# A two-layer recurrent and windowed-attention step on one core: input norm from a second copy of the input, sample states two slots earlier, fp32 scores, and sixteen low parts on another engine

## Chip, cores and metric

One core of one Trainium2 chip. The metric is the device time of one execution in microseconds (us), lower is better. Before the change the median of 3 runs is 1066.13 us (1063.52 to 1066.85).

## What is computed

A prompt of 1024 tokens and 8 single sample tokens (T = 1032 columns, 1024 features) go through two layers. Layer 1 is HGRN2, a gated linear recurrence with 8 heads of 128 x 128 state; layer 2 is attention over a window of 128 with 16 query heads, 2 key/value heads and learned sinks. Both have a SiLU gate path and a residual.

```python
u = _rmsnorm(h, norm_g) @ w_in
q, f, i, g = split(u)                       # layer 1
S = exp(b_end) * S + einsum(k * exp(b_end - b), v);  o = q_decayed @ S + masked(q k^T) v
h = h + (rmsnorm(o) * silu(g)) @ w_out
s = einsum(q, k) * scale                    # layer 2, banded blocks of 128 queries, 256 keys
m = max(max(s), sink);  p = exp(s - m);  o = p @ v / (sum(p) + exp(sink - m))
h = h + (o * silu(gate)) @ w_out2;  y = rmsnorm(h)
```

The outputs are y, the recurrent states of prompt and samples, and the last keys and values.

## The kernel before, in words

Features lie on the 128 partitions and tokens along them. A weight block of 128 x 1024 (`n`, 0 to 73) is multiplied with the stream in three units of 344 columns (`TU`), each unit in one PSUM bank. To keep fp32 accuracy at the speed of the one-pass type fp32r, weights and stream are each cut into a high part and a low part, and a unit is 24 products: 8 feature tiles times (high x high, high x low, low x high). The high part of a weight block is made on ACT (`prepare`, L782), the low part on POOL for early blocks (L643) and on DVE for late ones (L1095, L1100). The unit banks are G0 to G2; `start_unit` (L1582) waits until the former content of the bank was read (`unit_read`). The other five banks, R0 to R4, serve everything else.

Every engine runs a list written out by hand, and semaphores connect them. In the order of time:

**Start (0 to 39 us).** SP loads the input `x` in 8 feature tiles of 516 KB into A, weight blocks between them. For each tile ACT squares it (L878), PE sums the squares over the partitions by 3 plain fp32 products with a matrix of ones (L1691), DVE makes XH (L1220) and XL (L1222), and PE does the 9 products of block 0 (L1696). After the last tile ACT turns the sums into 1/rms, `RB` (L886, L889), and DVE multiplies each unit by it when it reads its bank (`evacuate`, L1103). So no bank of block 0 can be emptied, and block 1 can't start, before RB is there.

**Recurrence (39 to 475 us).** Iterations `it` = 0 to 8 of 9 slots, one unit per slot, while the recurrence of head it - 1 is worked on in the same slots: `diagonal`, six `level`s, transposes in slots 2 and 7, `chunk_sums` in slot 8 on PE. In slot 8 DVE runs `decode_state` (L1168: products of sample values and keys, its input read at a stride of 8 elements), `decode_add` (L1177) and then `chunk_states` (L1183: 8 dependent steps). Slot 0 of the next iteration has `head_output` (L1660) on PE, which needs those chunk states. The sample values are stored to DRAM by SP (L495) and read back to all partitions (L499). POOL decays the sample states in slot 4 (`decode_parts`, L677).

**Middle (475 to 784 us).** Gate blocks, output projection, residual, shared keys and values, queries with rotation. ACT makes KBH (L969) and DVE KBL (L1362), the high and low parts of the rotated keys.

**Attention (784 to 1001 us).** Steps s = -3 to 31; query group q is 2 head pairs x 128 queries. PE's order in a step is `values(s-1)`, `turn(s)`, `scores(s+2)`, then 17 products of gate blocks (s < 16) or 18 of the first half of the output projection (s from 16, L1842). ACT cuts the queries (L1002), DVE makes their low part (L1414), PE multiplies three fp32r combinations into two banks (L1788), using the upper and the lower 64 rows of the array for the two heads of a pair. DVE's `minima` (L1417) adds the mask, ACT takes the exponentials (L1009), DVE the denominators, POOL normalises (L716). For s from 17, `cut_slice` cuts the gated outputs of 16 groups: ACT the high part (L1025), DVE the low one (L1456).

**End (1001 to 1061 us).** Second half of the output projection, final norm, store.

Of the kernel before, what the change touches and what calls it, by code (L numbers as in the profile page):

```python
# [20 lines left out]
D = 1024  # L21
# [65 lines left out]
def unit_bank(u):  # L87

    return u % (2 if NU * N_B2 <= u < NU * N_BO else 3)
# [38 lines left out]
def build(nc, ctx, ins, outs):  # L128
# [3 lines left out]
    x_d, w_d, gain_d, lbl_d, st_d, lmask_d, imask_d, ident_d, cs_d, amask_d, smask_d, sink_d, sinks_d, kc_d, vc_d = ins  # L132
    y_d, stp_d, sts_d, kwin_d, vwin_d = outs
    h1_d = nc.dram_tensor("h1_spill", [P, KT, T], fp32, kind="Internal").ap()
    vs_d = nc.dram_tensor("sample_values", [HEADS, P, DEC], fp32, kind="Internal").ap()
# [54 lines left out]
    SQT = (VD, VK, KTT)  # L190
# [10 lines left out]
    KBH, KBL = sb("KBH", [P, SEQ], fp32r, rb_), sb("KBL", [P, SEQ], fp32r, rb_)  # L201
    rfree = [rb_[0]]
# [10 lines left out]
    QNH, QNL = sb("QNH", [P, 2, 2, P], fp32r, rb_), sb("QNL", [P, 2, 2, P], fp32r, rb_)  # L213
# [27 lines left out]
    R = [ctx.enter_context(nc.psum_tensor(f"R{i}", [P, 512], fp32)) for i in range(NBANK_R)]  # L241

# [8 lines left out]
    x_split = sem("x_split")  # L251
    sq_done = sem("sq_done")
    sq_used = sem("sq_used")
    ln_done = sem("ln_done")
    rb_done = sem("rb_done")
# [54 lines left out]
    kb_high = sem("kb_high")  # L310
# [32 lines left out]
    qn_high = sem("qn_high")  # L343
    qn_done = sem("qn_done")
# [111 lines left out]
    def _(sp):  # L456
# [10 lines left out]
        sp.dma_start(gain[:], gain_d).then_inc(const_in, 16)  # L467
        for k in range(KT):
            sp.dma_start(A[:, k, :], x_d[:, k, :]).then_inc(x_in[k], 16)
            if k < 3:  # L470
                load_weights(k)
            if k == 1:
# [19 lines left out]
        def sample_values(r):  # L492

            sp.wait_ge(unit_read, 9 * r + 9)
            sp.dma_start(vs_d[r], RAWV[:, SEQ:T]).then_inc(vs_out, 16)  # L495
            if r:
                sp.wait_ge(ss_prod, 2 * r)
            sp.wait_ge(vs_out, 16 * (r + 1))
            sp.dma_start(VD[:, 0:SEQ], vs_d[r].rearrange("e b -> (e b)").unsqueeze(0).broadcast_to([P, SEQ])  # L499
                         ).then_inc(vd_in, 16)  # L500
# [133 lines left out]
    def _(pool):  # L634
# [129 lines left out]
    def _(act):  # L764
# [31 lines left out]
        def gates(h):  # L796
# [10 lines left out]
            else:  # L807
                act.wait_ge(sq_used, KT)
# [65 lines left out]
        for k in range(KT):  # L874
            act.wait_ge(x_in[k], 16)
            if k >= 3:
                act.wait_ge(sq_used, k - 2)
# [3 lines left out]
        act.wait_ge(lbl_diff, 1)  # L881
        nc.scalar.activation(lbw[:, 1], lbw[:, 1], ACT.Exp).then_inc(lbl_exp, 1)
        act.wait_ge(setup_dve, 1)
        act.wait_ge(sq_used, KT)
        for i in range(NU):
            ins = nc.scalar.activation(RB[:, seg(i)], R[i][:, 0:TU], ACT.Ln, scale=1.0 / D, bias=eps[:])  # L886
        ins.then_inc(ln_done, 1)
        act.wait_ge(ln_done, 1)
        nc.scalar.activation(RB[:], RB[:], ACT.Exp, scale=-0.5).then_inc(rb_done, 1)  # L889
        nc.scalar.preload_act_table_set("sigmoid_and_others")  # L890

        for it in range(HEADS + 1):
            p, r = it - 2, it - 1
            for slot in range(9):
                if slot % 3 == 0:
# [73 lines left out]
        nc.scalar.activation(KBH[:], KE[:, 0:SEQ], ACT.Copy).then_inc(kb_high, 1)  # L969
# [25 lines left out]

        def cut_queries(q):

            if q == 0:
                act.wait_ge(q_rot, HP)
            if q >= 2:  # L1000
                act.wait_ge(sc_done, 2 * (q - 1))
            nc.scalar.activation(QNH[:, q % 2], pair(A, q), ACT.Copy, scale=-1.0).then_inc(qn_high, 1)  # L1002
# [24 lines left out]
        for s in range(-3, NQ + 1):  # L1027
            if 0 <= s < NQ:
                copy_before(s)
            if s + 3 < NQ:  # L1030
                cut_queries(s + 3)
# [60 lines left out]
    def _(dve):  # L1092
# [10 lines left out]
        def evacuate(u, i, dst):  # L1103
            dve.wait_ge(unit_done, u + 1)
            nc.vector.tensor_tensor(dst[:, seg(i)], G[i][:, 0:TU], RB[:, seg(i)], ALU.mult).then_inc(unit_read, 1)  # L1105
# [62 lines left out]
        def decode_state(r):  # L1168
            for i in range(2):
# [3 lines left out]
                                        VD[:, 0:SEQ].rearrange("p (e b) -> p b e", b=DEC)[:, 4 * i:4 * i + 4],  # L1173
# [39 lines left out]
        nc.vector.memset(ones[:], 1.0)  # L1213
        nc.vector.memset(eps[:], EPS).then_inc(setup_dve, 1)
        nc.vector.memset(AT[:], 0.0).then_inc(setup_dve, 1)
        dve.wait_ge(const_in, 16)
        for k in range(KT):
            g = gain[:, GAIN_A, k:k + 1]
            dve.wait_ge(x_in[k], 16)
            nc.vector.tensor_scalar(XH[:, k, :], A[:, k, :], g, None, ALU.mult).then_inc(x_split, 1)  # L1220
            dve.wait_ge(x_split, 2 * k + 1)
            nc.vector.scalar_tensor_tensor(XL[:, k, :], A[:, k, :], g, XH[:, k, :].bitcast(fp32), ALU.mult, ALU.subtract  # L1222
                                           ).then_inc(x_split, 1)
# [10 lines left out]
        dve.wait_ge(rb_done, 1)  # L1234
# [3 lines left out]
        for it in range(HEADS + 1):  # L1238
            r = it - 1
            for slot in range(9):  # L1240
# [10 lines left out]
                if r >= 0:  # L1251
# [109 lines left out]
        dve.wait_ge(kb_high, 1)  # L1361
        nc.vector.tensor_tensor(KBL[:], KE[:, 0:SEQ], KBH[:].bitcast(fp32), ALU.subtract).then_inc(kb_done, 1)  # L1362
# [48 lines left out]
        def cut_queries(q):  # L1411

            dve.wait_ge(qn_high, q + 1)
# [564 lines left out]
```

## Time and profile before

| | |
|---|---|
| median of 3 runs | 1066.13 us |
| profiled execution | 1063.2 us, its span 1061.4 us |
| PE busy | 1010.1 us, 95% of the span |
| DVE / POOL / ACT busy | 631.4 / 428.8 / 386.8 us |
| mean granted TensorE clock | 0.991 of full |

In the profile PE is TensorE's matmuls, PEld its weight loads, DVE the vector engine, ACT the scalar engine, POOL GpSimd, SP the queue that issues DMAs. A plain fp32 matmul shows as two instructions, an fp32r one as one. L1592 is a line of the kernel before. Idle time in brackets stands with the engine that ended it.

### The profile page before, as it was taken

The page shows a single profiled execution, that of the slowest core. Times are in us where ns is not written, and L with a number is a line of the kernel's source. Part 1 is how long each engine was busy: PE and PEld are TensorE (multiplying, and loading weights), DVE is VectorE, ACT ScalarE, POOL GpSimd, SP SyncE. Part 2 cuts the span into 40 slices and gives each one's busy share as a digit, 9 for nine tenths or more (in the row PEclk, how much of TensorE's full clock was granted, in tenths as well). Part 3 has the DMA queues.
Part 4 walks back from the last instruction along what each step waited for, and adds up shares of the span by engine and source line. Part 5 has one row for each costly group of instructions (what it writes and reads, how often), then busy time and mean ns, then how long its engine had stood idle before and what let it go on. Part 6 is the DMA issues. An engine that isn't in the chain of part 4 may idle for free.

```text
span 1061.4 us, 22401 instructions
## 1 busy us (share of the span) xinstructions
PE 1010.1 (95%) x9360; PEld 944.2 (89%) x9360; DVE 631.4 (59%) x1195; ACT 386.8 (36%) x775; POOL 428.8 (40%) x286
## 2 busy tenths in 40 slices
PE   6999999999999999999999999999989999898996
PEld 4899999999999998899999999999988888777895
DVE  8153746555564737456743234367667878977835
ACT  4412313132313133545332233510047757654522
POOL 1244545545545454612135342344535334322243
PEclk9999999999999999999999999999989989999998
DMA  7111213030312222012233324211112113322103
GB/s 284 41 61 41 86 39 104 21 104 24 102 63 64 71 73 83 22 43 63 103 105 136 120 80 145 77 46 58 40 57 63 59 56 101 91 71 61 50 34 127
DMA packets 50533, 81.39 MB, mean 77 GB/s; under 512 B 15425, under 2 KB 34433, under 8 KB 50305
## 3 DMA queue, kind: packets, MB, share of 16 engines
q1 hardware_dynamic: 50432, 79.97, 23.1%
q8 instruction: 74, 1.21, 0.5%
q14 instruction: 27, 0.21, 0.1%
HBM read 62.35 MB, written 17.60 MB: 75 GB/s over the span
## 4 chain that ended last, share of the span: by engine, by line
PE 71%; DVE 15%; ACT 7%; issue 5%; POOL 1%; DMA 0%; DVEq 0%; SPq 0%; ACTq 0%; POOLq 0%
PE G L1592 51%; PE G L1842 5%; DVE SP L1429 4%; ACT SP L1009 4%; PE R L1645 3%; DVE VK L1172 3%; DVE QNL L1414 3%; PE R L1691 2%; PE R L1619 1%; PE R L1684 1%; PE R L1670 1%; DVE PT L1447 1%; PE R L1667 1%; PE G L1696 1%; PE R L1631 1%
## 5 line engine op out<-in xcount | busy, mean ns | idle before, releaser
L1592 PE MATMUL G<-XH,WH 128*128 128x344 f32 x1176 | 385.8, 328 | 1.9 <-DVE RAWF L1105 1.9
L1592 PE MATMUL G<-XL,WH 128*128 128x344 f32 x1176 | 378.0, 321 | 2.4 <-DVE KE L1399 1.9
L1592 PE MATMUL G<-XH,WL 128*128 128x344 f32 x744 | 237.7, 319 | 0.0
L1592 PEld LDWEIGHTS G<-XH,WH 128*128 128x128 f32 x1176 | 221.9, 189 | 6.0 <-issue 2.4
L1592 PEld LDWEIGHTS G<-XL,WH 128*128 128x128 f32 x1176 | 221.7, 189 | 5.0 <-DVE WL L1095 2.2
L643 POOL TENSOR_TENSOR WL<-WR,WH 128x1024 fp32r<-128x1024 f32 x40 | 104.3, 2608 | 178.8 <-ACT WH L782 178.8
L782 ACT ACTIVATE WH<-WR 128x1024 fp32r<-128x1024 f32 x58 | 61.1, 1055 | 261.1 <-PE G L1592 166.7
L1592 PEld LDWEIGHTS G<-XH,WL 128*128 128x128 f32 x744 | 139.8, 188 | 0.0
L1592 PE MATMUL G<-XL,WL 128*128 128x344 f32 x432 | 139.2, 322 | 0.0
L674 POOL TENSOR_TENSOR K<-K,FP 128x512 f32<-128x512 f32 x48 | 78.1, 1627 | 104.6 <-PE R L1645 104.6
L720 POOL TENSOR_TENSOR SP<-SP,small 128x1024 f32<-128x1024 f32 (+1 forms) x32 | 57.3, 1792 | 135.1 <-DVE small L1440 135.1
L1009 ACT ACTIVATE SP<-SP,small 128x256 f32<-128x256 f32 (+1 forms) x128 | 61.8, 484 | 68.0 <-DVE small L1429 68.0
L1592 PEld LDWEIGHTS G<-XL,WL 128*128 128x128 f32 x432 | 81.9, 190 | 0.4
L1105 DVE TENSOR_TENSOR RAWQ<-G,RB 128x344 f32<-128x344 f32 x27 | 14.0, 517 | 79.7 <-PE G L1592 79.7
L1592 PE MATMUL G<-GR,WL 128*128 128x344 f32 x192 | 61.4, 320 | 0.0
L1592 PE MATMUL G<-GR,WH 128*128 128x344 f32 x192 | 61.4, 320 | 0.0
L1592 PE MATMUL G<-AR,WH 128*128 128x344 f32 x192 | 61.3, 319 | 0.0
L1105 DVE TENSOR_TENSOR RAWV<-G,RB 128x344 f32<-128x344 f32 x27 | 14.0, 517 | 77.4 <-PE G L1592 77.4
L1429 DVE CUSTOM_DVE_ANT_0 SP<-R,amask,sink 128x256 f32<-128x256 f32 (+1 forms) x128 | 51.9, 457 | 1.7 <-PE R L1788 1.7
L1842 PE MATMUL G<-XL,WH 128*128 128x344 f32 x144 | 47.9, 333 | 0.8 <-DVE AR L1549 0.8
L736 POOL TENSOR_TENSOR KE<-KE,CS 128x1032 f32<-128x1032 f32 x8 | 27.2, 3395 | 48.0 <-DVE KE L1403 48.0
L1842 PE MATMUL G<-XL,WL 128*128 128x344 f32 x144 | 46.0, 319 | 0.0
(251 smaller groups left out, 1940.6 us busy)
## 6 DMA issues: line engine op xcount, KB each, us to landing
WR<-w SPq DMA_DIRECT2D x58, 512.0 KB, 3.5
A<-x SPq DMA_DIRECT2D x8, 516.0 KB, 8.6
RESO<-x SPq DMA_DIRECT2D x8, 516.0 KB, 4.6
h_spill<-H SPq DMA_DIRECT2D x8, 516.0 KB, 2.9
gate_spill<-EV SPq DMA_DIRECT2D x24, 172.0 KB, 1.9
RES<-h_spill SPq DMA_DIRECT2D x24, 172.0 KB, 2.6
y<-H SPq DMA_DIRECT2D x24, 172.0 KB, 1.9
SS<-states SPq DMA_DIRECT2D x8, 512.0 KB, 5.0
```

Source lines behind the costliest of these rows:

```text
L643: nc.gpsimd.tensor_tensor(WL[:, n % 3], WR[:, n % 3], WH[:, n % 3].bitcast(fp32), ALU.subtract).then_inc(lo_pool, 1)
L674: nc.gpsimd.tensor_tensor(low, low, decay(l, 1).unsqueeze(2).broadcast_to([P, SEQ // (2 * h), h]), ALU.mult).then_inc(upd_k, 1)
L720: nc.gpsimd.tensor_tensor(sp_, sp_, small[:, q % 2, 4, :].unsqueeze(2).broadcast_to([P, 4, keys.stop - keys.start]), ALU.mult).then_inc(p_ ...
L782: nc.scalar.activation(WH[:, n % 3], WR[:, n % 3], ACT.Copy).then_inc(hi_done, 1)
L1009: nc.scalar.activation(SP_[q % 2][:, i, keys], SP_[q % 2][:, i, keys], ACT.Exp, bias=sm[:, 0, i:i + 1], scale=-1.0, accum_out=sm[:, 2, i:i ...
L1105: nc.vector.tensor_tensor(dst[:, seg(i)], G[i][:, 0:TU], RB[:, seg(i)], ALU.mult).then_inc(unit_read, 1)
L1172: nc.vector.tensor_tensor(VK[:, half(i)].rearrange("p (b e) -> p b e", b=4), VD[:, 0:SEQ].rearrange("p (e b) -> p b e", b=DEC)[:, 4 * i:4 ...
L1414: nc.vector.scalar_tensor_tensor(QNL[:, q % 2], pair(A, q), -1.0, QNH[:, q % 2].bitcast(fp32), ALU.mult, ALU.subtract).then_inc(qn_done, 1)
L1429: ins = nc.vector.tensor_tensor_reduce(out=SP_[q % 2][:, i, keys], in0=ps[:, keys], in1=amask[:, keys], scale=1.0, scalar=sink[:, h + i:h ...
L1592: return nc.tensor.matmul(G[unit_bank(NU * n + i)][:, 0:TU], w[:, n % 3, k, :], x[:, seg(i)], start=(k == 0 and p == 0), stop=(k == KT - 1 ...
L1645: ins = nc.tensor.matmul(b[v * w:v * w + w - h, first // 2:(first + w) // 2].rearrange("p (n h) -> p n h", h=h), K[r % 2][:, first:first + ...
L1842: return nc.tensor.matmul(G[unit_bank(u)][:, 0:TU], wt[:, k, :], x, start=(w == 0), stop=(w == 11))
```

## The change

- **Input norm.** A second, token-major copy of the input (`xt`, 8 tiles of 128 tokens x 1024, and `xs` for the samples) is loaded after the first. ACT squares each tile with a running sum along the row (one sum per token), then Ln and Exp give 1/rms with tokens on the partitions; PE's new `spread_scale` turns these 9 columns into rows on all partitions by 9 small fp32 products in slot 5 of iteration 0, and ACT copies them into RB. The 24 fp32 products with ones go. XH of tiles 1 to 7 moves from DVE to ACT. Weight block 0 is loaded ahead of the input, and PE starts when its high part is there; the low x high products run one tile later. Units 3 to 5 (block 1) go to R2 to R4 through the list `U`, so that they need no emptied bank.
- **Sample states.** `decode_state` and `decode_add` run in slot 6, `chunk_states` stays in slot 8 and comes first there. The sample values are stored transposed (pieces of 4 bytes) so that DVE reads them contiguously.
- **Scores.** One plain fp32 product per head in place of three fp32r ones, straight from the rotated queries and a negated copy of the keys (KNEG, made by ACT). The query cuts on ACT and DVE and KBL go.
- **Low parts.** `cut_slice`'s low part moves from DVE to POOL, behind `normalise` of the same step.

```diff
 def unit_bank(u):
+    if u < 2 * NU:
+        return u
@@ start, DMA queue
+        load_weights(0)
         for k in range(KT):
             sp.dma_start(A[:, k, :], x_d[:, k, :]).then_inc(x_in[k], 16)
-            if k < 3:
-                load_weights(k)
+        load_weights(1)
+        for c in range(NC):
+            sp.dma_start(XT[c][:, 0:D], xt_d[:, c]).then_inc(xt_in[c], 16)
+            if c == 3:
+                load_weights(2)
+        sp.dma_start(XS, xs_d).then_inc(xs_in, 16)
@@ sample_values
-            sp.dma_start(vs_d[r], RAWV[:, SEQ:T]).then_inc(vs_out, 16)
+            sp.dma_start(vs_d[r].rearrange("b e -> e b"), RAWV[:, SEQ:T], allow_slow_non_contiguous=True).then_inc(vs_out, 16)
@@ POOL, attention
-        for s in range(-3, NQ):
+        for s in range(-3, NQ + 1):
             if 0 <= s + 1 < NQ:
                 normalise(s + 1)
+            if s >= 17:
+                cut_slice(s - 1)
@@ ACT, start
-        for k in range(KT):
-            nc.scalar.activation(SQT[k % 3][:], A[:, k, :], ACT.Square).then_inc(sq_done, 1)
-            if k < 2:
-                prepare(k)
+        prepare(0)
+        for k in range(1, KT):
+            act.wait_ge(x_in[k], 16)
+            nc.scalar.activation(XH[:, k, :], A[:, k, :], ACT.Copy, scale=gain[:, GAIN_A, k:k + 1]).then_inc(x_hi_act, 1)
+        prepare(1)
+        for c in range(NC):
+            act.wait_ge(xt_in[c], 16)
+            nc.scalar.activation(XT[c][:, 0:D], XT[c][:, 0:D], ACT.Square, accum_out=SUM[:, c:c + 1]).then_inc(sq_done, 1)
+            if c == 0:
+                act.wait_ge(lbl_diff, 1)
+                nc.scalar.activation(lbw[:, 1], lbw[:, 1], ACT.Exp).then_inc(lbl_exp, 1)
+            if c == 5:
+                prepare(2)
...
+        nc.scalar.activation(SUM, SUM, ACT.Ln, scale=1.0 / D, bias=eps[:]).then_inc(ln_done, 1)
+        nc.scalar.activation(RSTD, SUM, ACT.Exp, scale=-0.5).then_inc(rstd_done, 1)
+        for i in range(2):
+            act.wait_ge(spread, i + 1)
+            nc.scalar.activation(RB[:, half(i)], R[i][:], ACT.Copy).then_inc(rb_done, 1)
@@ DVE, recurrence
                     if slot == 8:
+                        chunk_states(r)
+                    if slot == 6:
                         decode_state(r)
                         decode_add(r)
-                        chunk_states(r)
@@ PE, start
+        def spread_scale():
+            pe.wait_ge(rstd_done, 1)
+            pe.wait_ge(masks_in, 16 * 3)
+            for c in range(NC):
+                ins = nc.tensor.matmul(R[c // 4][:, (c % 4) * P:(c % 4 + 1) * P], RSTD[:, c:c + 1].broadcast_to([P, P]),
+                                       ident[:], start=True, stop=True)
...
+            pe.wait_ge(rb_done, 1)
+            nc.tensor.matmul(R[0][:, 0:DEC], RSTD[0:DEC, NC:NC + 1].broadcast_to([DEC, P]), ident[0:DEC, 0:DEC],
+                             start=True, stop=True).then_inc(spread, 1)
...
+                if it == 0 and slot == 5:
+                    spread_scale()
@@ PE, scores
-                for n, (a, k) in enumerate(((QNH, KBH), (QNH, KBL), (QNL, KBH))):
-                    for v in range(2):
-                        ins = nc.tensor.matmul(R[v][:, 2 * P * jj + keys.start:2 * P * (jj + 1)], a[rows, q % 2, jj, :],
-                                               k[rows, tok], start=(n == 0), stop=(n == 2))
+                for v in range(2):
+                    ins = nc.tensor.matmul(R[v][:, 2 * P * jj + keys.start:2 * P * (jj + 1)], pair(A, q)[rows, jj],
+                                           KNEG[rows, tok], start=True, stop=True)
```

## Rows read from the trace of the kernel before

**Rows 1.** The page, chain that ended last: shares of the span by engine and line.
```profile
PE G L1592 51%; PE G L1842 5%; DVE SP L1429 4%; ACT SP L1009 4%; PE R L1645 3%; DVE VK L1172 3%; DVE QNL L1414 3%; PE R L1691 2%; PE R L1619 1%; PE R L1684 1%; PE R L1670 1%; DVE PT L1447 1%; PE R L1667 1%; PE G L1696 1%; PE R L1631 1%
```
**Rows 2.** PE's waits: who for whom: us in total, times, longest.
```profile
PE R L1670 <- DVE ST L1192: 6.9, 8, 1.0
...
PE R L1788 <- DVE small L1429: 10.2, 13, 1.2
PE R L1788 <- DVE QNL L1414: 3.8, 1, 3.8
PE R L1815 <- DVE PT L1447: 1.6, 2, 1.0
PE G L1842 <- DVE AR L1549: 0.8, 1, 0.8
```
**Rows 3.** The chain in order of time, start-up: start us, us, what.
```profile
34.42 1.75 PE R L1691 x6
...
39.47 26.68 PE G L1592 x168
```
**Rows 4.** Timeline of the start: start us, us, engine, instruction, idle before it.
```profile
6.58 1.06 ACT L782 ACTIVATE WH<-WR 128x1024 fp32r<-128x1024 f32 x1 [0.23 <-DMA WR<-w]
...
10.26 2.56 POOL L643 TENSOR_TENSOR WL<-WR,WH 128x1024 fp32r<-128x1024 f32 x1 [0.20 <-ACT WH L782]
...
10.65 3.26 DVE L1222 SCALAR_TENSOR_TENSOR XL<-A,gain,XH 128x1032 fp32r<-128x1032 f32 x1
...
14.61 1.30 DVE L1222 SCALAR_TENSOR_TENSOR XL<-A,gain,XH 128x1032 fp32r<-128x1032 f32 x1
```
**Rows 5.** Stretches: busy of PE, PEld, DVE, ACT, POOL; PEclk, DMA share, GB/s.
```profile
10.00:12.00 2.00, 1.84 (x3) 1.17 (x4) 1.96 (x2) 1.24 (x2) 1.80 (x2) 1.00 1.04 422
...
38.00:40.00 2.00, 0.53 (x3) 0.56 (x4) 1.19 (x3) 1.98 (x2) 0.00 (x0) 1.00 0.00 0
...
780.00:784.00 4.00, 1.27 (x12) 1.27 (x12) 3.42 (x4) 2.24 (x5) 0.60 (x1) 0.77 0.01 2
```
**Rows 6.** Timeline around the end of iteration 4: DVE, then PE.
```profile
249.92 0.52 DVE L1105 TENSOR_TENSOR RAWV<-G,RB 128x344 f32<-128x344 f32 x1 [2.63 <-PE G L1592]
...
255.07 4.23 DVE L1172 TENSOR_TENSOR VK<-VD,K 128x512 f32<-128x512 f32 x2
259.34 1.89 DVE L1180 TENSOR_TENSOR SS<-SS,VK 128x1024 f32<-128x1024 f32 x1
...
261.46 2.72 DVE L1195 SCALAR_TENSOR_TENSOR ST<-ST,DECC,R 128x128 f32<-128x128 f32 x7
...
261.48 0.49 PE L1670 MATMUL R<-QU,ST 128*128 128x128 f32 x2 [0.94 <-DVE ST L1192]
```
**Rows 7.** Timeline of the same iteration: an issue of SP, and POOL in slot 4.
```profile
220.60 0.38 SPq L481 DMA_DIRECT2D SS<-states  x1
...
237.95 1.90 POOL L680 TENSOR_TENSOR SS<-SS,DECC 128x1024 f32<-128x1024 f32 x1
```
**Rows 8.** Timeline of one attention step, PE.
```profile
927.00 0.39 PE L1788 MATMUL R<-KBH,QNH 64*128 64x256 f32 x2 [0.79 <-DVE small L1429]
...
927.91 0.43 PE L1842 MATMUL G<-XL,WXH 128*128 128x344 f32 x1
...
930.94 1.08 PE L1815 MATMUL R<-PT,VP 128*64 128x256 f32 x8
931.95 1.09 PE L1800 MATMUL R<-ident,SP 128*128 128x128 f32 x8
```
**Rows 9.** Timeline of the same step, DVE.
```profile
930.32 1.42 DVE L1414 SCALAR_TENSOR_TENSOR QNL<-A,QNH 128x256 fp32r<-128x256 f32 x1
```
**Rows 10.** The chain in order of time, 784 us.
```profile
784.27 6.14 PE G L1592 x24
```
**Rows 11.** Weight loads of the recurrence by form: busy us, mean ns; idle before.
```profile
L1592 PEld LDWEIGHTS G<-XH,WH 128*128 128x128 f32 x577 | 108.5, 188 | 2.8 <-issue 0.2
...
L1667 PEld LDWEIGHTS R<-AT,VH 128*128 128x128 f32 x128 | 19.1, 191 | 0.0
```

More of the change, by code:

```diff
@@ L200, in build @@
     rb_ = [rest]
-    KBH, KBL = sb("KBH", [P, SEQ], fp32r, rb_), sb("KBL", [P, SEQ], fp32r, rb_)
-    rfree = [rb_[0]]
+    KNEG = sb("KNEG", [P, SEQ], fp32, rb_)
+    rb_[0] += 4 * SEQ
     rb_[0] += 2 * 4 * SEQ
@@ L212, in build @@
     PT = sb("PT", [P, 2, 512], fp32, rb_)
-    QNH, QNL = sb("QNH", [P, 2, 2, P], fp32r, rb_), sb("QNL", [P, 2, 2, P], fp32r, rb_)
+    rb_[0] += 2 * 4 * 4 * P
     SGR = sb("SGR", [P, 2, 2, P], fp32, rb_)
@@ L250, in build @@
     lb_done = sem("lb_done")
-    x_split = sem("x_split")
+    xt_in = [sem(f"xt_in{c}") for c in range(NC)]
+    xs_in = sem("xs_in")
+    x_hi_dve = sem("x_hi_dve")
+    x_hi_act = sem("x_hi_act")
+    x_lo = sem("x_lo")
     sq_done = sem("sq_done")
-    sq_used = sem("sq_used")
     ln_done = sem("ln_done")
+    rstd_done = sem("rstd_done")
+    spread = sem("spread")
     rb_done = sem("rb_done")
@@ L872, in gate_sigmoid @@
             nc.scalar.activation(SG[m % 2][:], GT[m][:], ACT.Sigmoid).then_inc(g_sig, 1)
[L874 removed]
+        prepare(0)
+        act.wait_ge(const_in, 16)
+        for k in range(1, KT):
             act.wait_ge(x_in[k], 16)
[L876 to L889 removed]
+            nc.scalar.activation(XH[:, k, :], A[:, k, :], ACT.Copy, scale=gain[:, GAIN_A, k:k + 1]).then_inc(x_hi_act, 1)
+        prepare(1)
+        act.wait_ge(setup_dve, 1)
+        for c in range(NC):
[6 more added lines that the diff above has]
+                prepare(2)
+        act.wait_ge(xs_in, 16)
+        nc.scalar.activation(XS, XS, ACT.Square, accum_out=SUM[0:DEC, NC:NC + 1]).then_inc(sq_done, 1)
+        act.wait_ge(sq_done, NC + 1)
+        nc.scalar.activation(SUM, SUM, ACT.Ln, scale=1.0 / D, bias=eps[:]).then_inc(ln_done, 1)
+        act.wait_ge(ln_done, 1)
+        nc.scalar.activation(RSTD, SUM, ACT.Exp, scale=-0.5).then_inc(rstd_done, 1)
+        for i in range(2):
+            act.wait_ge(spread, i + 1)
+            nc.scalar.activation(RB[:, half(i)], R[i][:], ACT.Copy).then_inc(rb_done, 1)
+        act.wait_ge(spread, 3)
+        nc.scalar.activation(RB[:, SEQ:T], R[0][:, 0:DEC], ACT.Copy).then_inc(rb_done, 1)
         nc.scalar.preload_act_table_set("sigmoid_and_others")
@@ L894, in _ @@
             for slot in range(9):
-                if slot % 3 == 0:
+                if slot % 3 == 0 and (it or slot):
                     prepare(3 * it + slot // 3 + 2)
@@ L968, in _ @@
         act.wait_ge(k_rot, 1)
-        nc.scalar.activation(KBH[:], KE[:, 0:SEQ], ACT.Copy).then_inc(kb_high, 1)
+        nc.scalar.activation(KNEG[:], KE[:, 0:SEQ], ACT.Copy, scale=-1.0).then_inc(kb_done, 1)
         for i in range(2):
@@ L994, in _ @@
             prepare(N_BQ + j + 2)
[L996 to L1002, printed above, removed]
         def exponentials(q):
@@ L1409, in _ @@
         dve.wait_ge(q_rot, HP)
-        def cut_queries(q):
-            dve.wait_ge(qn_high, q + 1)
-            nc.vector.scalar_tensor_tensor(QNL[:, q % 2], pair(A, q), -1.0, QNH[:, q % 2].bitcast(fp32), ALU.mult,
-                                           ALU.subtract).then_inc(qn_done, 1)
         def minima(q):
@@ L1684, in head_sums @@
                 nc.tensor.matmul(b[:, 0:TU], ones[:], SQN[:, seg(i)], start=True, stop=True).then_inc(group_done, 1)
+        def spread_scale():
[4 more added lines that the diff above has]
+                                       ident[:], start=True, stop=True)
+                if c % 4 == 3:
+                    ins.then_inc(spread, 1)
+            pe.wait_ge(rb_done, 1)
+            nc.tensor.matmul(R[0][:, 0:DEC], RSTD[0:DEC, NC:NC + 1].broadcast_to([DEC, P]), ident[0:DEC, 0:DEC],
+                             start=True, stop=True).then_inc(spread, 1)
         pe.wait_ge(setup_dve, 1)
-        pe.wait_ge(*lo_value(0))
+        pe.wait_ge(hi_done, 1)
         for k in range(KT):
-            pe.wait_ge(sq_done, k + 1)
+            pe.wait_ge(x_lo, k + 1)
             for i in range(NU):
-                ins = nc.tensor.matmul(R[i][:, 0:TU], ones[:], SQT[k % 3][:, seg(i)], start=(k == 0), stop=(k == KT - 1))
-            ins.then_inc(sq_used, 1)
-            pe.wait_ge(x_split, 2 * k + 2)
-            for i in range(NU):
-                for p, (w, x) in enumerate(((WH, XH), (WH, XL), (WL, XH))):
-                    ins = nc.tensor.matmul(G[i][:, 0:TU], w[:, 0, k, :], x[:, k, seg(i)],
-                                           start=(k == 0 and p == 0), stop=(k == KT - 1 and p == 2))
-                if k == KT - 1:
-                    ins.then_inc(unit_done, 1)
+                for p in range(2):
+                    product(0, i, k, p)
+            if k == 1:
+                pe.wait_ge(*lo_value(0))
+            if k:
+                for i in range(NU):
+                    product(0, i, k - 1, 2)
+        for i in range(NU):
+            product(0, i, KT - 1, 2).then_inc(unit_done, 1)
         for it in range(HEADS + 1):
```

66 lines of the change are left out of this document (32 added, 34 removed).

## Prediction

> **What bounds the kernel now.** I read the page's chain first [rows 1]: the three-product units on PE (L1592, L1842) hold 56% of the span, so PE's own work is most of it, and time can be won only where PE idles, where its clock is low, or where its work shrinks. PE's waits [rows 2] then name the idle places that this change touches: 6.9 us in 8 waits of `head_output` for the first chunk state, 10.2 us before the scores for `minima`, 1.6 us for a copy of turned probabilities, 0.8 us for a low part, and 3.8 us once before the first scores. The start is the last place: PE has 8 groups of fp32 sums there, each like the last one, 1.75 us, and from its end at 36.17 us to 39.47 us PE stands still while ACT makes RB [rows 3].
>
> **Part 1, the start.** I compare when unit 6, the first of block 2, can begin. Before: 39.47 us plus units 3, 4, 5. Seven units take 26.68 us [rows 3], 3.81 each, 0.159 per product, so 50.9 us.
>
> After, one step behind the other. Weight block 0 comes first, the input tile second, so both are there when the first two were before, near 6.5 us [rows 4]. A tile of 516 KB at 422 GB/s [rows 5] takes 1.25 us; DVE's low part takes 1.30 us, and 3.26 us when POOL's low part of a weight block runs beside it (10.65 beside 10.26) [rows 4]. Eight low parts with their gaps are 10.6 us, the first high part 0.75 (an estimate from the length of the same tile), and POOL's two weight blocks each add 2.0: 6.55 + 15.4 = 22.0 us. ACT's high parts, 1.07 to 1.2 us a tile, keep ahead of that. PE has 9 products, 1.43 us, per tile and follows; 12 products are left after the last tile, so block 0 ends at 23.9 us. Units 3 and 4 go into free banks and end at 31.5 us.
>
> RB now hangs on ACT. After the input DVE clears AT and subtracts the small table (1.1 us, an estimate from the 1.30 us of a low part), so ACT passes its wait behind the first square at about 23.3 us. Seven squares with a running sum (1.16 each, by the 1.06 us of a copy of 1024 columns [rows 4] and a tenth for the sum), a weight block (1.06), the sample tile (1.16) and Ln and Exp (0.6) make 10.9 us: 34.2 us. The token-major tiles are no later than that: 9.99 MB stand before the end of the last one, 24 us at 422 GB/s, done at 26 us. So PE idles from 31.5 to 34.2 us, then has 8 small fp32 products of 128 columns (0.22 each by the sums' 0.58 for 344), a wait for ACT's first copy that ends with them, and one tiny product: 36.3 us. Unit 5 ends at 40.1 us, and unit 6 begins: its bank was read long before. **Gain 10.8 us.** From here on iteration 0 has its old order; POOL's and ACT's work for blocks 3 to 5 hangs on PE's units and moves with them.
> Bounds: if ACT never waits for the table, PE is never short and unit 6 starts at 35 us, gain 15.9. If DVE is 3 us later than worked out and the clock is lost in the new idle time (below, 2.4 us), gain 5.4.
>
> **Part 2, sample states.** At the end of iteration 4 DVE spends 4.23 us on the strided products and 1.89 us on the sum before its eight chunk states (a copy, then 2.72 us), and PE waits 0.94 us [rows 6]. With them gone from slot 8, the states start at 255.2 us and end at 258.2 us, before PE ends the next unit at 259.9 us. The wait goes in all 8 iterations: **gain 6.9 us** [rows 2]. What is late next is `diagonal`, which waits for a product of DVE that itself waits for PE; that does not move. In slot 6 DVE idles 2.63 us [rows 6]; contiguous products would take 0.6 us each (half of the 1.30 us of 1032 columns [rows 4]), with 1.2 to 1.9 us for the sum, 2.4 to 3.1 in all: at most 0.5 us late for the next evacuation, which three banks cover. If that cover were gone each iteration would lose the 0.5 us, 4 us. The scattered store is SP's: behind it stand the read-back and the load of the states (220.60), whose user is POOL at 237.95 [rows 7]. Some 17 us lie between, and a load of this size (tile of 516 KB, 1.25 us by the rate) needs a third of them at most: 12 us are free. A store in pieces of 4 bytes shows in no row; I cost it at nothing up to those 12 us.
>
> **Part 3, scores and low parts.** In a step of the second half of this stage PE's groups are scores 0.91 us (927.00 to 927.91), products to 930.94, values 1.01, transposes 1.09, together 6.04 us, and a wait of 0.79 us for DVE: a period of 6.83 us [rows 8]. DVE's ring is: `minima`, wait for ACT's exponentials, denominators, gate, copy, QNL 1.42 us [rows 9], low part, next `minima`. The last two before it go, and the ring falls below 5.41 us, less than PE's 6.04. So PE's waits for DVE in this stage, 10.2 + 1.6 + 0.8 = 12.6 us [rows 2], go; I leave 2 us of them at the two ends: **gain 10.6 us** (12.6 less 2). POOL gets a product of 256 columns behind its normalising; POOL idles over half of the step, and the reader of the low part comes 15 us later.
> The new score group is 4 plain fp32 matmuls of 256 columns on 64 rows each. No row shows such a shape. Nearest are the values: 4 fp32 matmuls of 256 columns in tiles of 64 columns, 8 instructions, 931.95 - 930.94 = 1.01 us [rows 8], which is two at a time: one alone is 0.43 us by the sums, three of 344 columns in 1.75 us [rows 3]. Scores now run two heads at a time as well: 12 instructions in 0.91 us. I take 1.01 for 28 groups (+2.8 us) and half of it for the 4 with 128 keys (-1.6): **loss 1.2 us**. Bounds: below nothing, -2 us, if the mode changes cost less too; and 1.72 us a group if the row halves don't overlap in fp32, a loss of some 21 us.
> The first scores need the last rotated query alone, not its two cuts: **gain 1.0 us** of the 3.8 us wait. In that wait the granted clock falls from 2.4 to 1.2 GHz (0.77 over 780 to 784) [rows 5], and the next unit takes 6.14 us [rows 10] in place of 3.81. PE's idle time of 3.3 us around 38 us left the clock at 1.00 [rows 5]. The new one is 2.8 us, so I take it that the clock stays: **gain 2.4 us** (from 0). KBL goes from DVE at a time when PE runs on, at no gain.
> A rule speaks against the fp32 scores. Fp32 weights of 128 columns load in 191 ns, those of fp32r in 188 [rows 11], and either is hidden behind the matmul before it. The Trainium skill (TensorE: Matmul & The Clock Gate, section on weight-path modes) says that the fast load is on for 128 weights only if the type isn't fp32, and gives about 2x as measured. By it the 8 loads of a group would cost twice as much, an estimate of 1.5 us more a group if nothing hid them. I go by the rows.
>
> **Sum**, against the profiled execution of 1063.2 us (span 1061.4): -10.8 - 6.9 - 10.6 + 1.2 - 1.0 - 2.4 = -30.5, 1032.7 us. The median of the runs shown, 1066.13, lies 2.9 above that execution; on its scale it is 1035.6. I say 1035.
>
> **Rivals.**
> (a) The row halves take turns in fp32: a score group costs 1.72 us. PE is then the bound of every step with 6.85 us (6.04 + 0.81), the idle time is still gone, and about 20 us come back: 1055 us. For it: no row has this shape. Against: the row halves overlap in fp32r, column halves in fp32 [rows 8]. 12%.
> (b) The start pays less, because ACT and DVE are later than worked out or the clock falls in the new idle time: 1041 us. For it: ACT's chain is long and has only estimates for the running sum. 12%.
> (c) The other side: in fp32 neither half of the rows overlaps, nor is a load hidden behind the matmul before it. A group is then 8 loads of 0.19 us and 8 half-matmuls of 0.22 us, 3.2 us, 2.3 more in 32 groups: +72 us, 1105 us. It ends slower from 1.9 us a group on (0.91 plus 31.7 us over 32). Its place would be the score groups alone. 3%.
> (d) Sample states come late: the scattered store takes over 12 us, POOL waits in slot 4, and each us beyond costs 8: at 2 us beyond 1051 us. For it: no row has pieces of 4 bytes. Against: 12 us are free [rows 7]. 3%.
> (e) DVE's freed time doesn't reach PE, since POOL's products delay DVE: a low part of DVE took 3.26 us beside POOL against 1.30 alone [rows 4], and QNL starts while POOL normalises. But `minima` and the copy read PSUM, and PE has 0.6 us to spare against the ring; half of the 10.6 us would be lost, 1040 us. 7%.
> (f) All three gains are hidden by something that I didn't see: no change, 1%.
>
> **How the numbers follow.** The forecast has 62%, and its own range is 1026 to 1044 (the bounds of part 1, the clock, 2.6 us of scatter between runs). With (b), (e) and a part of (d) the range of 8 in 10 is 1024 to 1052; (a) and (c) are mostly left out. A measurement of this kernel tells 0.3%, about 3 us, from no change. Slower by that: (c) and half of the rest of doubt, 4%. Within it: 2%. Faster: 94%.
>
> **What would show it.** Right: unit 6 begins near 40 us, with an idle time of 2 to 3 us ahead of the small products; no wait of L1670's counterpart; score groups of 1.0 us at a period of 6.1 us and no waits for `minima`; granted clock 1.00 at 784 us. Wrong: score groups of 1.7 us or more; PE short before block 1; a wait of DVE in slot 6 for the read-back; idle time of the same length ended by another engine.

## The result and the profile after

The changed kernel takes **1054.16 us** (median of 4 runs, 1051.98 to 1057.27) beside 1066.35 for the kernel before on the same chip: ratio 0.9905, 95% interval 0.9885 to 0.9925. That is faster, but by 1% and not by the 3% that I forecast, and it lies outside my range on the high side. (The quotient of the two medians is 0.989.) The profiled execution, the slowest of the four, took 1057.27 us with a span of 1055.5, against 1061.4 before.

PE's waits in the kernel after, the answer to [rows 2] (columns as there):

```profile
PE R L1652 <- issue: 10.7, 8, 2.5
PE G L1598 <- DVE XL L1243: 10.3, 1, 10.3
PE G L1598 <- issue: 4.6, 6, 1.6
PE R L1638 <- issue: 4.0, 8, 1.5
PE R L1811 <- DVE A L1429: 2.9, 1, 2.9
PE R L1691 <- ACT K L867: 2.2, 1, 2.2
```

The row of 10.3 us is the time before PE's first product. The waits for the first chunk state, for `minima` and for the copy of probabilities are gone, as forecast. In their place stand 15.3 us of "issue" in L1652 (the level products) and L1598 (the three-product units): idle time before an instruction that waited for nothing the profile shows. Before, their counterparts (L1645, L1592) had no such row. L1691 (head sums) waits once for ACT, which is new too.

Three marks cut the span: the first `diagonal` product, the first scores, and the end.

| | before | after | difference | forecast |
|---|---|---|---|---|
| start of the span to the first `diagonal` | 67.66 | 55.20 | -12.5 | -10.8 |
| from there to the first scores | 715.07 | 731.89 | **+16.8** | -7.9 |
| from there to the end | 278.7 | 268.4 | -10.3 | -11.8 |

So the start and the attention stage did what they were to do, and the recurrence took it back. The start, from the chain in order of time of the kernel after, answers to [rows 3]:

```profile
12.89 16.50 DMA VH<-xt
29.42 1.15 ACT VH L901 x2
...
32.24 2.05 PE R L1698 x16
...
34.61 3.98 PE R L1598 x24
38.59 15.11 PE G L1598 x96
```

PE's wait for Ln and Exp is down to 0.6 us, and unit 6 begins at 38.59 us. The chain now starts from the last token-major tile, which lands at 29.4 us; ACT waited 0.75 us for it.

One attention step, the chain of the kernel after, answers to [rows 8]:

```profile
927.96 1.06 PE R L1811 x8
929.02 3.02 PE G L1865 x18
...
934.09 1.06 PE R L1811 x8
```

A score group takes 1.06 us, a step 6.13, and PE idles nowhere in it. The recurrence is where to look. This is its chain over two slots of one iteration:

```profile
206.17 0.89 PE R L1638 x63
207.05 4.04 PE G L1598 x24
211.09 0.88 issue
211.97 0.72 PE R L1652 x48
212.69 3.98 PE G L1598 x24
...
218.35 0.63 PE G L1598 x4
218.98 1.64 issue
220.63 3.30 PE G L1598 x20
```

A unit waits for semaphores only ahead of its first product, yet here one stands still for 1.64 us between its fourth and fifth product. POOL stands still in these slots too. Its product that waits for `diagonal` could start when that ended, at 207.1 us, and started at 210.34 (POOL's timeline; in the version below without the scattered store it starts 0.1 us behind `diagonal`):

```profile
210.34 1.53 POOL L686 TENSOR_TENSOR K<-K,FG 128x512 f32<-128x512 f32 x1 [6.83 <-remote]
```

SP's issues around it, in the kernel after:

```profile
201.76 0.79 SPq L507 DMA_DIRECT2D sample_values<-RAWV  x1
211.71 0.32 SPq L511 DMA_DIRECT2D VD<-sample_values  x1
```

The store of the sample values, whose pieces are now 4 bytes, is the one transfer between: 10 us pass until SP may read back. And the stretches of that time (columns as in [rows 5]):

```profile
204.00:206.00 2.00, 1.81 (x28) 1.42 (x26) 0.63 (x2) 0.81 (x3) 0.00 (x0) 1.00 0.76 184
206.00:208.00 2.00, 1.83 (x70) 1.80 (x71) 1.97 (x5) 0.26 (x1) 0.00 (x0) 1.00 0.00 0
...
210.00:212.00 2.00, 1.12 (x12) 0.83 (x11) 1.50 (x4) 0.00 (x0) 1.53 (x1) 1.00 0.00 0
```

The records of the transfers end by 206 us, the store's semaphore comes at 211.7, and PE and POOL lose time in between, PE again at 219 us. That is the suspicion which the runs test.

The stalls cost more than their own length. In the recurrence of the kernel after, the granted clock fell from 2.4 to 1.2 GHz four times, at 162.0, 264.4, 319.0 and 370.2 us, for 3.4 us each, each time within 1.1 us of the end of such a stall. The first of these stretches, behind a stall that ended at 161.2 us:

```profile
162.00:166.00 4.00, 4.00 (x17) 4.00 (x18) 1.86 (x2) 0.00 (x0) 1.81 (x1) 0.57 0.90 262
```

The seven periods from `diagonal` to `diagonal` are 48.9, 50.4, 51.6, 51.1, 52.3, 53.4 and 52.2 us after, and 49.5 each before. In sum they take 360.0 us after and 346.4 before.

### The profile page after: what moved, and what is told of

The parts are those of the page before. It is cut to its first block, busy times and chain, and to the rows that moved or that the text cites. A ratio compares the mean times of both kernels' runs of the same rounds, so it can differ in the third digit from the quotient of the medians.

```text
span 1055.5 us, 22018 instructions
## 1 busy us (share of the span) xinstructions
PE 1008.5 (96%) x9202; PEld 941.9 (89%) x9202; DVE 563.6 (53%) x1140; ACT 386.8 (37%) x761; POOL 425.8 (40%) x302
## 4 chain that ended last, share of the span: by engine, by line
PE 87%; ACT 3%; issue 3%; DVE 2%; DMA 2%; POOL 1%; SPq 1%; DVEq 0%; POOLq 0%
PE G L1598 57%; PE G L1865 9%; PE R L1652 3%; PE R L1811 3%; PE R L1838 3%; PE R L1823 3%; DMA VH<-xt 2%; PE R L1626 1%; PE R L1674 1%; PE R L1663 1%; PE R L1677 1%; PE R L1691 1%; PE R L1638 1%; POOL WR L649 1%; SPq L482 1%
## 5 line engine op out<-in xcount | busy, mean ns | idle before, releaser
L1598 PE MATMUL G<-XH,WH 128*128 128x344 f32 x1176 | 390.4, 332 | 12.0 <-DVE XL L1243 10.3
L1598 PE MATMUL G<-XL,WH 128*128 128x344 f32 x1176 | 381.8, 325 | 4.9 <-issue 2.6
L1598 PEld LDWEIGHTS G<-XH,WH 128*128 128x128 f32 x1176 | 225.3, 192 | 17.0 <-issue 14.2
L1598 PE MATMUL G<-XH,WL 128*128 128x344 f32 x744 | 237.4, 323 | 0.3 <-issue 0.3
L1598 PEld LDWEIGHTS G<-XL,WH 128*128 128x128 f32 x1176 | 225.3, 192 | 6.8 <-issue 3.6
L1598 PEld LDWEIGHTS G<-XH,WL 128*128 128x128 f32 x744 | 141.4, 191 | 3.1 <-issue 3.0
L1598 PE MATMUL G<-XL,WL 128*128 128x344 f32 x432 | 140.0, 324 | 0.0
L1598 PEld LDWEIGHTS G<-XL,WL 128*128 128x128 f32 x432 | 82.6, 191 | 0.9 <-issue 0.7
L1598 PE MATMUL G<-AR,WH 128*128 128x344 f32 x192 | 61.3, 319 | 0.0
L1598 PE MATMUL G<-GR,WH 128*128 128x344 f32 x192 | 61.3, 319 | 0.0
L1598 PE MATMUL G<-GR,WL 128*128 128x344 f32 x192 | 61.3, 319 | 0.0
L1444 DVE CUSTOM_DVE_ANT_0 SP<-R,amask,sink 128x256 f32<-128x256 f32 (+1 forms) x128 | 52.2, 463 | 12.9 <-PE R L1811 12.5
L1652 PEld LDWEIGHTS R<-QU,K 128*30 128x30 f32 (+5 forms) x2432 | 33.5, 107 | 21.7 <-issue 21.6
L1123 DVE TENSOR_TENSOR RAWQ<-G,RB 128x344 f32<-128x344 f32 x24 | 12.4, 516 | 71.7 <-PE G L1598 71.7
L1652 PE MATMUL R<-QU,K 128*30 128x16 f32 (+5 forms) x2432 | 38.6, 187 | 10.7 <-issue 10.7
L748 POOL TENSOR_TENSOR KE<-KE,CS 128x1032 f32<-128x1032 f32 x8 | 27.2, 3395 | 49.5 <-DVE KE L1424 49.5
```

The lines of the kernel that those rows point to most:

```text
L1444: ins = nc.vector.tensor_tensor_reduce(out=SP_[q % 2][:, i, keys], in0=ps[:, keys], in1=amask[:, keys], scale=1.0, scalar=sink[:, h + i:h ...
L1598: return nc.tensor.matmul(U[unit_bank(NU * n + i)][:, 0:TU], w[:, n % 3, k, :], x[:, seg(i)], start=(k == 0 and p == 0), stop=(k == KT - 1 ...
L1652: ins = nc.tensor.matmul(b[v * w:v * w + w - h, first // 2:(first + w) // 2].rearrange("p (n h) -> p n h", h=h), K[r % 2][:, first:first + ...
```

## The experiments

**The 32-byte store.** Theory A: the store in pieces of 4 bytes holds back instructions of all engines. Everything else of the change stays, the values are stored as before, and DVE reads them with a stride, still in slot 6.

```diff
-            sp.dma_start(vs_d[r].rearrange("b e -> e b"), RAWV[:, SEQ:T], allow_slow_non_contiguous=True)
+            sp.dma_start(vs_d[r], RAWV[:, SEQ:T])
...
-                                        VD[:, half(i)].rearrange("p (b e) -> p b e", b=4),
+                                        VD[:, 0:SEQ].rearrange("p (e b) -> p b e", b=DEC)[:, 4 * i:4 * i + 4],
```

> The changed kernel with the store of sample values in pieces of 32 bytes and the strided products of before, still in slot 6. Theory A (the store in pieces of 4 bytes, 10 us long, holds back the fetching of instructions, which the trace shows as waits called issue in the middle of units): the waits of PE called issue in the recurrence fall from some 15 us to about 4 (those ahead of the diagonal), an iteration takes 48.6 us, and the time is 1034 us. Theory B (the move of decode_state to slot 6 itself delays PE): the strided products take 6.1 us there in place of 2.7, so the waits stay or grow, 1055 us or more. Theory C (the new order at the start shifts what is fetched when): no change, 1054 us.

Measured: 1034.77 us (1032.81 to 1036.88), ratio 0.9728 [0.9712, 0.9745]. PE's waits in it:

```profile
PE G L1598 <- DVE XL L1243: 10.3, 1, 10.3
PE R L1638 <- issue: 4.0, 8, 1.5
PE R L1691 <- ACT K L867: 3.1, 1, 3.1
PE R L1811 <- DVE A L1429: 2.9, 1, 2.9
```

The "issue" rows of L1652 and L1598 are gone, and every period is 48.27 to 48.30 us, 338.0 in sum. One store was worth some 20 us. The periods are 22.0 us shorter in sum than in the kernel after. PE's stalls in them there add up to 14.6 us; four falls of the clock, at half the speed for 3.4 us, are another 6.8 us (an estimate from those lengths): 21.4 together. SP reads back 4.1 us after the store's issue in that iteration (3.3 to 4.6 in the eight).

**The scattered store alone**, in the kernel before: the same diff the other way round, with the decode left in slot 8.

> The kernel before with the store in pieces of 4 bytes and contiguous products alone, still in slot 8. Theory A: 6.9 us are won, since the chunk states begin 3.4 us earlier, and some 20 us are lost to late instructions: about 1079 us, with waits called issue in each iteration. Theories B and C: the win alone, 1059 us.

Measured: 1066.97 us (10 runs, 1061.25 to 1073.27), ratio 1.0041 [1.0017, 1.0065]; the profiled execution is the slowest of the ten, its span 1071.4 against 1061.4. It has a new row:

```profile
PE R L1645 <- issue: 11.3, 8, 2.0
```

The direction is A's, and the row is the one of the kernel after; the size is not. The median is 4 us slower where I expected 16, and the runs scatter over 12 us. The gain that I expected is there: PE's 6.9 us of waits for the first chunk state are not in this version's list, since the contiguous products are shorter and lie ahead of them. So the store costs about 11 us here by the medians, less than the 20 in the kernel after, and some 17 in the profiled execution (10.0 us of span and the 6.9): 11.3 of stalls and three falls of the clock. Why it is less I can't say.

**A scratch store nobody waits for.** To the 32-byte version comes a second store of the same values, in 4-byte pieces, into scratch memory; only the end of the kernel and the next overwriting of its source, most of an iteration later, wait for it.

```diff
+            sp.dma_start(du_d[r].rearrange("b e -> e b"), RAWV[:, SEQ:T], allow_slow_non_contiguous=True).then_inc(v_out, 16)
```

> e1 with one more store in pieces of 4 bytes per head, to a scratch tensor, issued behind the read-back; nothing on the way to the result waits for it, save the overwriting of its source a slot cycle later. Theory A: the late instructions come back whole, some 20 us above e1. Rival A2 (what hurt was that SP stood waiting for the long store, so that the read-back and the load of the states were late): as e1, within 3 us.

Measured: 1062.56 us (9 runs, 1058.14 to 1071.38), ratio 1.0001 [0.9966, 1.0036], 28 us above the version without it. Its row in PE's waits:

```profile
PE R L1655 <- issue: 18.2, 11, 3.4
```

So it isn't that SP or DVE wait for the values. The store itself does the harm, as A says. (DVE's wait ahead of the overwriting is no other cause: it stands in the same place in the versions with 8-byte pieces below, which lose nothing.)

**What about the store does it: four more versions** of the 32-byte kernel, each with one more transfer of small pieces per iteration. First the same 1024 values in 512 pieces of 8 bytes:

```diff
+            sp.dma_start(du_d[r].rearrange("j e i -> e j i"), RAWV[:, SEQ:T].rearrange("e (j i) -> e j i", i=2),
+                         allow_slow_non_contiguous=True).then_inc(v_out, 16)
```

> As e3 (e1 and a scratch store behind the read-back), but in 512 pieces of 8 bytes in place of 1024 of 4. If the price goes with the number of pieces: half of e3's 28 us above e1, 1048 us. If it goes with the bytes or with there being one more store at all: as e3, 1062 us. If pieces of 8 bytes are no longer slow: as e1, 1035 us.

Measured: 1036.38 us, ratio 0.9718 [0.9692, 0.9744]: nothing lost. Then a second read of the sample outputs in 1024 pieces of 4 bytes:

```diff
+            sp.dma_start(QS[:, p, 0, :], os_d[p].rearrange("n e -> e n"), allow_slow_non_contiguous=True).then_inc(os_in, 16)
```

> e1 with the read of sample outputs, 1024 pieces of 4 bytes from DRAM, issued twice (the second into a tile that is free there). It lands in 2.3 us where the store took 10. If small pieces as such hold back instructions: 10 us or more above e1. If only slow stores do: within 3 us of e1, 1035 us.

Measured: 1033.13 us, ratio 0.9708 [0.9678, 0.9738]: nothing lost. That left two explanations for the first of them, the size of a piece and their number, so I set 512 stored pieces of 4 bytes (`RAWV[:, SEQ:SEQ + 4]`) against 1024 of 8 bytes (`RAWV[:, T - 16:T]`, in pairs):

> The kernel with the 32-byte store (1034.8 us, ratio 0.9728) and a scratch store for which only the end waits, of 512 pieces of 4 bytes (half of the samples). If the size of a piece is what hurts: about half of the 28 us that 1024 such pieces cost, 1046 to 1050 us, ratio 0.984 to 0.988. If it was the number of pieces above some 512 that hurt: no change, as with 512 pieces of 8 bytes, ratio 0.971 to 0.973.

> The same with a scratch store of 1024 pieces of 8 bytes. If the size of a piece is what hurts: no change, ratio 0.971 to 0.973, 1031 to 1036 us. If the number of pieces is what hurts: +20 to 28 us, ratio 0.991 to 0.999.

Measured: 1058.07 us (1056.61 to 1060.12), ratio 0.9949 [0.9931, 0.9967] with 512 of 4 bytes; 1034.4 us (1032.29 to 1038.86), ratio 0.9737 [0.9706, 0.9769] with 1024 of 8. The page's line on packets shows the pairs. 512 pieces of 8 bytes, then of 4, have the same count; so have 1024 pieces of 8 bytes and of 4 (the last two lines):

```profile
DMA packets 55922, 85.63 MB, mean 83 GB/s; under 512 B 19784, under 2 KB 38792, under 8 KB 55696
```

```profile
DMA packets 55922, 85.61 MB, mean 81 GB/s; under 512 B 19784, under 2 KB 38792, under 8 KB 55696
```

```profile
DMA packets 60018, 85.66 MB, mean 83 GB/s; under 512 B 23880, under 2 KB 42888, under 8 KB 59792
```

```profile
DMA packets 60018, 85.63 MB, mean 81 GB/s; under 512 B 23880, under 2 KB 42888, under 8 KB 59792
```

Stored pieces of 8 bytes cost nothing, be they 512 or 1024; stored pieces of 4 bytes cost 23 us (1058.07 - 1034.77) when 512 and 28 when 1024. It is the size, and of the two directions tried only the store. My "about half" for 512 was wrong: what is lost is not in proportion to the count.

**The scores alone**, in the kernel before: fp32 products from the rotated queries and negated keys, without the cuts; the low parts of the output stay on DVE.

```diff
-                for n, (a, k) in enumerate(((QNH, KBH), (QNH, KBL), (QNL, KBH))):
-                    for v in range(2):
+                for v in range(2):
...
-            if s + 3 < NQ:
-                cut_queries(s + 3)
```

> The kernel before with the fp32 scores alone; the low parts stay on DVE. In the changed kernel a score group takes 1.07 us and the waits for minima are gone. If DVE's ring was the bound because of QNL, the period of the second half falls from 6.83 to about 6.2 us and the stage ends some 9 to 10 us earlier: 1054 us. If both QNL and the low part have to go before the ring is shorter than PE's work, less than half of that: 1059 us or more.

**The low parts alone**, in the kernel before: `cut_slice`'s subtraction moves from DVE to POOL and nothing else.

> The kernel before with the late low parts on POOL alone. By the ring, 0.41 us go in each of some 15 steps whose period is set by it: 5 to 6 us, 1058 us. If POOL's work beside DVE's stretches QNL by as much, no change.

Measured: 1055.2 us, ratio 0.9907 [0.9885, 0.9929], for the scores; 1061.06 us, ratio 0.9957 [0.9943, 0.9971], for the low parts. PE's wait for `minima`, 10.2 us before, is 3.0 in the first (L1766) and 6.0 in the second (L1789):

```profile
PE R L1766 <- DVE small L1408: 3.0, 10, 0.5
```

```profile
PE R L1789 <- DVE small L1437: 6.0, 11, 0.9
```

Each helps, the low parts by the 5 us expected; neither removes the wait. By my working the scores alone should have. Their 1055.2 us lie near the 1054 that I expected by that working, but not for its reason: the step is 6.49 us and not 6.2, and in this trace two falls of the clock (at 782 and 857 us) lasted 3.4 us each where those of the kernel before lasted 6.8.

**A version that beats both.** To the 32-byte version: 48 instead of 36 gate products before the first scores' place in the order, so that PE has half a unit more to do while DVE ends the first rotation (and 66 instead of 60 for the next step).

```diff
-    return (36, 60, 90)[s + 3] if s < 0 else min(360, 90 + 270 * (s + 1) // 16)
+    return (48, 66, 90)[s + 3] if s < 0 else min(360, 90 + 270 * (s + 1) // 16)
```

> e1 with 48 in place of 36 products of gate blocks ahead of the first scores (and 66 for 60 in the step after). PE's wait for the last rotated query, 2.9 us, shrinks to 1 us; if the clock is lost by the length of that idle time, the granted clock stays at 1.00 there: 1.9 + 2.4 = 4 us under e1. If the clock falls for another reason (little work in the scores that follow), 2 us under e1.

Measured: **1031.25 us** (1030.78 to 1032.42), ratio 0.9703 [0.9688, 0.9717], the fastest of all and 3.5 us under the 32-byte version, where I expected 4. The wait before the first scores is 1.0 us. Its effect on the clock is read from the stretch that holds this wait, first in the 32-byte version, then in this one:

```profile
764.00:768.00 4.00, 1.14 (x9) 0.94 (x8) 3.97 (x3) 1.62 (x3) 1.73 (x1) 0.76 0.00 0
```

```profile
764.00:768.00 4.00, 3.02 (x23) 2.61 (x22) 3.97 (x4) 1.86 (x3) 1.49 (x1) 1.00 0.00 0
```

The granted clock fell from 2.4 to 1.2 GHz behind the 2.9 us and stayed at 2.4 with 1.0. From the first scores to the end are 264.0 us instead of 268.2; 1.9 of these 4.2 us are the 12 products that now stand ahead of that mark (0.159 us each).

**Best, with the low parts on DVE again.**

> The best version (32-byte store, input norm, fp32 scores, gates filled at 48, 66, 90; ratio 0.9703 to before) with the low parts back on DVE. Theory: once QNL (1.42 us) is gone from DVE's ring, the ring is below PE's 6.13 us whoever makes the low part, so POOL's part of the change gives nothing beside the fp32 scores: ratio 0.970 to 0.971 (1031 to 1032 us), no waits for minima. Rival: the two add up as they did alone (0.9% and 0.4%), so that some 3 to 5 us come back: ratio 0.974 or more, with waits of the scores for minima.

Measured: 1036.14 us (1035.81 to 1038.08), ratio 0.9745 [0.9729, 0.9761]: the rival, almost 5 us. The step is 6.50 us, and DVE's timeline shows why:

```profile
907.66 0.68 DVE L1454 COPY PT<-R 128x512 f32<-128x512 f32 x1
908.26 1.41 DVE L1465 TENSOR_TENSOR AR<-A,XL 128x256 fp32r<-128x256 f32 x1
909.60 0.47 DVE L1436 CUSTOM_DVE_ANT_0 SP<-R,amask,sink 128x256 f32<-128x256 f32 x1
```

```profile
907.50 1.89 POOL L732 TENSOR_TENSOR SP<-SP,small 128x1024 f32<-128x1024 f32 x1 [4.60 <-DVE small L1447]
```

In the kernel before QNL took 1.42 us at this place [rows 9] and the low part behind it 0.41 (931.66). Without QNL the low part takes QNL's place beside POOL's normalising, and its time: 1.41 us. Whichever of the two stands there, it ends 0.28 us behind POOL's instruction: here at 909.67 behind 909.39, QNL in the kernel before at 931.74 behind 931.46. So removing either of the two takes away only the 0.41 us behind POOL and shortens the step from 6.83 to 6.49 us; removing both brings it to PE's 6.13.

**Best, with the decode in slot 8 again**, ahead of the chunk states, and the products strided.

> The best version with the sample states' decode back in slot 8, ahead of the chunk states. Theory: PE waits about 0.9 us for the first chunk state in each of 8 iterations again, +7 us: ratio 0.977 (1038 us), and the row of PE waiting for ST is back with 6 to 8 us in 8 waits. Rival: the move was worth nothing, since another stall takes the place of this wait: ratio 0.970, 1031 us.

Measured: 1035.47 us (1034.91 to 1036.38), ratio 0.9736 [0.9721, 0.975]. The wait is back in full, but only 4.2 us come with it:

```profile
PE R L1676 <- DVE ST L1210: 6.9, 8, 1.0
```

Its periods are 49.5 us against 48.27: slot 6 gains 1.2 us in each. But after the last `diagonal` slot 6 loses 5.6 us: 373.4 us to the first scores against 367.8. Three things make that up. The first is the new row of L1691 [PE's waits, above]. The chain of the best version in the last iteration:

```profile
434.59 2.28 DVE VK L1190 x2
...
436.89 1.23 DVE SS L1198
438.12 1.22 DVE A L1219
...
439.36 1.43 ACT FG L879 x3
...
441.78 1.06 ACT K L867
...
442.88 1.13 PE R L1691 x3
```

Behind the decode on DVE waits the scaling of a head's output (L1219), behind that ACT's norm of the next head, and behind that PE's head sums: 3.1 us, once, since only the last iteration has these norms. The second is the clock. PE waits 1.9 us for the rotated keys near 677 us in every version; in this version's trace the clock fell to 1.2 GHz for 3.4 us behind that, in the slot-8 one it did not (0.69 here, 1.00 there):

```profile
678.00:682.00 4.00, 4.00 (x20) 4.00 (x19) 2.35 (x2) 0.00 (x0) 2.74 (x1) 0.69 0.28 107
```

```profile
676.00:680.00 4.00, 3.14 (x20) 2.85 (x19) 0.76 (x1) 1.06 (x1) 2.02 (x2) 1.00 0.12 44
```

At half the speed that is 1.7 us (an estimate from the 3.4). It isn't the doing of slot 6: behind this wait the clock fell in 7 of the 14 traces, with either slot. The third is one stall of 1.15 us marked "issue" (L1652, at 399 us), in a version without the 4-byte store. Together these are 5.9 us, less 0.3 of a wait for the chunk state that the slot-8 version has there.

## Why the prediction was wrong

**Part 2 failed, at the scattered store.** I wrote: "A store in pieces of 4 bytes shows in no row; I cost it at nothing up to those 12 us." SP could read back 9.7 to 12.4 us after its issue, and POOL never waited for its states, so by that working it was free. It cost 20 us all the same: 1054.16 against 1034.77 with the one line changed. Rival (d) named the store, but with another mechanism, POOL waiting for late states; POOL's decode was never late. That its 1051 us and the 1055 of rival (a) lie near the measured time is chance. What is lost is instructions that start late on engines with no part in the transfer, which the scratch store shows by itself. I bounded the latency and gave the transfer no other way to cost anything. Shown: the stalls of PE add up to 11 to 19 us with 4-byte stored pieces and to 1.2 us at most without them (the 1.5 and 0.4 us ahead of each `diagonal`, which every version has, left out); they wait for no semaphore, fall inside a unit, and hit PE and POOL alike. Only argued: how. The page lists instruction queues among the DMA queues (q8 and q14, with 98 packets), so a held-up fetch of instructions would fit. The traces support it: in the iteration above the only queue with packets from 206 to 218 us is q1, and PE's stall inside the unit ends behind a packet of q8 that starts at 218.3; the 32-byte version has two of q8 in the same stretch of its iteration (200 to 212 us). The DMA views of these stretches, after and 32-byte:

```profile
q1 hardware_dynamic: 274, 1.02, 27.4%
```

```profile
q1 hardware_dynamic: 288, 1.05, 27.7%
q8 instruction: 2, 0.03, 1.2%
```

No run isolates it, so the way stays open.

**Part 2's own gain** came in each iteration, but was not kept whole: the 6.9 us of waits went, and in the 32-byte version the periods fell by 1.2 us each, 8.4 in the seven. The products took 1.52 us and the sum 1.22, inside my 2.4 to 3.1, and no evacuation in slot 6 cost PE anything. What I missed is what is queued behind the decode on DVE in the last iteration: 3.1 us of head sums (2.2 in the kernel after), and in five of the eight traces with the 3.1 a fall of the clock behind them. I had looked at the next evacuation only.

**Part 1** was right and under-booked, 12.5 us for 10.8. I had ACT end at 34.2 us, from a chain that waited for DVE's small table until 23.3; the table came at 20.9, since DVE's low parts ended at 18.6 and not at 22.0, and PE's small products began at 32.24. PE's end of unit 4 was right, 31.6 for 31.5. The last transfer of the copy, which I had at 26 us by a rate of 422 GB/s, ended at 29.4 and cost ACT 0.75 us. Rival (b) fell.

**Part 3.** The score group measured 1.06 to 1.07 us for my 1.01; the 28 full groups cost some 1.5 us more than booked. Rivals (a) and (c) fell: two row halves do run together in fp32 (1.06 us, not 1.72). The rule of the Trainium skill (TensorE: Matmul & The Clock Gate, section on weight-path perf modes) that I had weighed, a fast load only for types other than fp32, doesn't show between fp32 and fp32r: the fp32 loads of the scores take 187 ns at the median (L1811), those in fp32r took 183 to 186. The waits for DVE went, but for a reason that was half wrong. I took QNL out of DVE's ring and left everything else its length, and so had "below 5.41"; with the scores alone, or with the low parts on DVE in the best version, the ring is 6.5 us, since the low part grows from 0.41 to 1.41 us. Rival (e), which said that a collision with POOL eats the gain, is this mechanism; the change escapes it because it moves both.

**The clock** did not stay, and this 2.4 us term failed too: behind the wait of 2.86 us the granted clock was at the lower level from before 788 to after 792 us, and the unit took 6.32 us. I had taken 3.3 us of idle time at the start as proof that 2.8 us are safe. They are not, nor always 1.9. And I had no term for the clock that stalls in the recurrence take. The best version gets this term, with 1.0 us.

**The sum.** On the traces, the 32-byte version stands 26.3 us below the kernel before, where I had 30.5: -12.6 at the start, -3.3 to the first scores (8.4 in seven periods, 1.0 before the first scores and 0.3 in the last iteration, less 3.1 of head sums and 3.4 for two falls of the clock, behind them and near 677 us, an estimate), -10.4 after. The kernel after has the same start and end, and 20.1 us more between: 22.0 in the periods, less 1.9 behind them.

## What to carry to other kernels

A transfer is not priced by its size and its landing alone: where stored pieces are as small as 4 bytes, measure it, and look for idle time marked "issue" inside groups of instructions that wait for nothing. If a scatter is needed, put the stride on the engine's reads, or make a piece 8 bytes. When work moves on an in-order engine, follow the queue behind it in every kind of iteration, the last one too; and when an instruction leaves a place that it shared with POOL, price what moves up into that place at the duration it will have there.

## What was not expected of the hardware

- A store of 4 KB in 1024 pieces of 4 bytes was waited for 9.9 us after its issue (201.76 to 211.71), the same bytes in 128 pieces of 32 bytes 4.1 us (195.53 to 199.62). Eight of the former lengthened this kernel by 20 us and, added to the 32-byte version as scratch stores, by 28; nine runs of the latter scatter over 13 us, where 18 of the kernel before lie within 3.7.
- 512 pieces of 4 bytes cost 23 us, 1024 pieces of 8 bytes nothing, nor did 1024 reads of 4 bytes.
- A subtraction of DVE on 256 columns took 0.41 us, and 1.41 when a POOL product of 1024 columns was running: it ended 0.28 us behind POOL's.
- An idle time of PE of 2.9 us ahead of the first scores lowered the granted clock in each of eight traces (the kernel after, the fp32 scores alone, and six with the 32-byte store), one of 1.0 us there in none of three. One of 3.1 us ahead of the head sums lowered it in 5 of 8, one of 1.9 us for the rotated keys in 7 of 14, so the length of the idle time alone doesn't decide it in these rows.
- In each of the 14 traces the granted clock also fell once between 837 and 869 us. In the kernel after, this fall began at 861.7 us with no idle time of PE since the first scores; PE was in a run of products of 16 columns for the samples (L1920, L1921).
